# Waits by bank at two stages, cross attention reordered, cached rotary keys turned by VectorE, and another order of ScalarE's splits in each block's first span

## What is computed

```python
xp = xp + 0.5 * swiglu_ffn(xp, ffn1_norm, ffn1_w_gate, ffn1_w_up, ffn1_w_down)      # D_FF = 2816
q_lat, q_rope, c_kv, k_rope, u = mixer_project(xp, pos_p, mix_norm, w_in, ...)       # input projection
o_lat = mla_attend(q_lat, q_rope, pos_p, ((c_kv, k_rope, pos_p),))                   # 8 heads, latent 256, rope 32
xp = xp + mix_output(o_lat, u_ext, w_v_up, conv_w, conv_b, conv_ln_g, conv_ln_b, w_out)
...
past_c = cache_kv_latent[page_table].reshape(8, 4096, 256)      # paged cache of the decode requests
past_kr = cache_k_rope[page_table].reshape(8, 4096, 32)         # rotary keys of the cache
# scores of a decode step: q_lat . c + q_rope . kr, over 4096 cached and 4 new keys
s = (einsum('bqhc,btc->bhqt', ql, c) + einsum('bqhr,btr->bhqt', qr, kr)) * ATTN_SCALE
...
xp = xp + cross_attend(xp, cross_norm, w_cq, mk, mv, w_co)      # 4 heads of 256; decode rows use cached mem_k, mem_v
xp = xp + 0.5 * swiglu_ffn(xp, ffn2_norm, ffn2_w_gate, ffn2_w_up, ffn2_w_down)
y = rmsnorm(xp, final_norm)
```

## Time and profile before

| what | value |
|---|---|
| median of three runs | 2448.7 us (2446.03 to 2457.05) |
| the profiled execution's own time | 2448.1 us |
| its span | 2446.3 us |
| TensorE busy | 2393.6 us (98%) |
| TensorE weight loads busy | 2250.0 us (92%) |
| VectorE busy | 1462.0 us (60%) |
| ScalarE busy | 953.6 us (39%) |
| GpSimd busy | 1149.6 us (47%) |
| mean granted TensorE clock | 0.995 |

### The profile page before, as it was taken

One profiled execution on the slowest core, in us unless ns is written; L12 is line 12 of the kernel. 1 busy time (PEld: TensorE's weight loads), 2 busy tenths in 40 slices (PEclk: granted clock), 3 DMA queues, 4 the chain that ended last, 5 costly groups with the idle time before them and its releaser, 6 DMA issues.

```text
span 2446.3 us, 48239 instructions
## 1 busy us (share of the span) xinstructions
PE 2393.6 (98%) x18415; PEld 2250.0 (92%) x18415; DVE 1462.0 (60%) x2672; ACT 953.6 (39%) x2015; POOL 1149.6 (47%) x832
## 2 busy tenths in 40 slices
PE   7999999999999999999999999999999999999998
PEld 7999999999999888666677999789999999999998
DVE  6644545468784756866777761444654545456786
ACT  7323333343332334666443330432532333334335
POOL 2647777787833251002212422013465777777770
PEclk9999999999999999999999999999999999999999
DMA  4112323245423123006564312431112232325432
GB/s 127 35 53 92 104 91 104 91 150 163 123 60 120 47 60 98 1 1 267 198 247 122 122 43 77 154 106 47 41 53 61 87 109 86 109 86 170 141 105 80
DMA packets 191279, 246.57 MB, mean 101 GB/s; under 512 B 9768, under 2 KB 152457, under 8 KB 186262
## 3 DMA queue, kind: packets, MB, share of 16 engines
q1 hardware_dynamic: 187007, 205.11, 27.0%
q0 software_dynamic: 3584, 37.75, 3.9%
q10 hardware_dynamic: 543, 1.69, 0.2%
HBM read 197.93 MB, written 42.80 MB: 98 GB/s over the span
## 4 chain that ended last, share of the span: by engine, by line
PE 58%; DVE 3%; ACT 1%; issue 1%; POOL 0%; ACTq 0%; DVEq 0%
PE ps L1445 6%; PE ps L1440 6%; PE ps L1444 6%; PE ps L422 4%; PE ps L425 4%; PE ps L426 4%; PE ps L2785 3%; PE ps L1547 2%; PE ps L1551 2%; PE ps L1550 2%; PE ps L2815 2%; PE ps L2830 1%; PE ps L2797 1%; PE ps L3155 1%; PE ps L3009 1%; PE ps L3135 1%
## 5 line engine op out<-in xcount | busy, mean ns | idle before, releaser
L1440 PE MATMUL ps<-op_hi_S,home_hi 128*128 128x264 f32 x1280 | 364.2, 285 | 0.0
L1445 PE MATMUL ps<-op_hi_S,home_lo 128*128 128x264 f32 x1280 | 364.0, 284 | 0.0
L1444 PE MATMUL ps<-op_lo_S,home_hi 128*128 128x264 f32 x1280 | 363.6, 284 | 0.0
L1838 DVE TENSOR_TENSOR ps<-st_copy,ps 128x264 f32<-128x264 f32 x196 | 85.6, 437 | 333.5 <-PE ps L1445 294.1
L1440 PE MATMUL ps<-op_hi_A,home_hi 128*128 128x264 f32 x960 | 273.4, 285 | 0.0
L1444 PE MATMUL ps<-op_lo_A,home_hi 128*128 128x264 f32 x960 | 272.9, 284 | 0.0
L1445 PE MATMUL ps<-op_hi_A,home_lo 128*128 128x264 f32 x960 | 272.8, 284 | 0.0
L2447 POOL CAST w_hi<-w_raw 128x1024 fp32r<-128x1024 f32 x40 | 49.0, 1224 | 431.7 <-PE ps L422 146.9
L1975 POOL TENSOR_TENSOR home_lo<-home_v,home_hi 128x512 fp32r<-128x512 f32 x160 | 212.2, 1337 | 74.3 <-ACT home_hi L1567 74.3
L1445 PEld LDWEIGHTS ps<-op_hi_S,home_lo 128*128 128x128 f32 x1280 | 240.9, 188 | 0.0
L1444 PEld LDWEIGHTS ps<-op_lo_S,home_hi 128*128 128x128 f32 x1280 | 240.9, 188 | 0.0
(11 more groups left out here) (444 smaller groups left out, 6518.0 us busy)
## 6 DMA issues: line engine op xcount, KB each, us to landing
g_v<-g_keep SPq DMA_DIRECT2D x56, 528.0 KB, 3.7
f_raw<-in_ffn_w_gate SPq DMA_DIRECT2D x44, 512.0 KB, 4.0
f_raw<-in_ffn_w_up SPq DMA_DIRECT2D x44, 512.0 KB, 4.1
g_keep<-st SPq DMA_DIRECT2D x16, 1320.0 KB, 6.0
f_raw<-in_ffn_w_down SPq DMA_DIRECT2D x28, 512.0 KB, 3.9
g_keep<-st SPq DMA_DIRECT2D x16, 528.0 KB, 2.7
span_raw<-in_ffn_w_down SPq DMA_DIRECT2D x16, 512.0 KB, 5.6
ring<-in_cache_mem_k SPq DMA_DIRECT2D x16, 512.0 KB, 4.2
```

The source lines that it names most:

```text
L1440: mm = pe.matmul(out, w, xhi[:, k, q], start=self.STARTS[unit] and k == 0, stop=False, skip_group_check=True)
L1444: pe.matmul(out, w, xlo[:, k, q], start=False, stop=False, skip_group_check=True)
L1445: mm = pe.matmul(out, lo, xhi[:, k, q], start=False, stop=self.STOPS[unit] and k == KH - 1, skip_group_check=True)
L1838: dve.tensor_tensor(out, a, b, op).then_inc(self.evicted, 1)
```

## The change

Five edits.

1. First span of each FFN: ScalarE makes g_hi of product 3 before the two span_hi splits, and stays one product ahead in span 0; VectorE makes g_lo of product 3 behind the seventh tile of product 0 instead of behind the fourth.
2. The first units of the input projection wait, tile by tile, for the last add on the bank that they use.
3. The first units of the query projection do likewise.
4. Cross attention starts with the scores of steps 0 and 1, each waiting for less, and turns the first probabilities between the two halves of c_turned(0). At the end, the transposes of co_s come ahead of x_values(15), which goes to bank 5.
5. In decode attention, VectorE transposes kr_nat in 32x32 blocks into kr_t, of which there are two; the group of TensorE transposes and its ScalarE copy go. A block transpose leaves the positions in another layout, so the rope scores are 16 matmuls of 128 columns instead of four of 512.

```diff
-        TURNS = 9
-        TURN_OF = [(0, 0), (0, 1), (0, 2), (0, 3), None, (1, 0), (1, 1), (1, 2), (1, 3)]
+        TURNS = 8
+        TURN_OF = [(ch, j) for ch in range(2) for j in range(4)]
...
+        def rope_turned(h):
+            return v_dve, QT + h + 1
...
+        def x_bank(j):
+            return 5 if j == X_STEPS - 1 else 3
...
+            def last_of_bank(self, bank):
+                return self.tile_added(self.LAST, max(i for i in range(self.N_TILES) if self.TILE_BANKS[i] == bank))
...
                     if last:
+                        operand_high(0, 3)
                         span_high(0, 4)
                         span_high(0, 5)
...
-                        if p < 4:
+                        if p < 3 and first:
+                            operand_high(q, p + 4)
+                        elif p < 4 and not first:
                             operand_high(q, p + 3)
-                        elif not last:
+                        elif p >= 4 and not last:
                             operand_high(q + 1, p - 4)
...
-                            if j == 4 and p < 4:
+                            if p < 4 and j == (7 if first and p == 0 else 4):
                                 operand_low(q, p + 3)
...
+            def second_taken(self, mb, tt):
+                return self.taken, self.o + 2 * NTT + NTT * KC + NTT * mb + tt + 1
...
                 if h >= 2:
-                    pool.wait_ge(turned_pe, TURNS * (h - 2) + 5)
+                    pool.wait_ge(*rope_turned(h - 2))
...
-                    pe.wait_ge(z_dve, NTT * (2 * m + s) + tt + 1)
+                    if m == 0:
+                        pe.wait_ge(*ffn1.last_of_bank(NTT * s + tt))
+                    else:
+                        pe.wait_ge(z_dve, NTT * (2 * m + s) + tt + 1)
...
-                for part, turns in enumerate(((0, 1, 2, 3), (4,), (5, 6, 7, 8))):
-                    for i in turns:
+                rope = kr_t[h % 2][:, :].rearrange("p (n j x) -> p j n x", n=4, j=4)
+                for ch in range(2):
+                    for i in range(4 * ch, 4 * ch + 4):
                         pe.wait_ge(*key_turn_taken(h, i))
                     for j in range(4):
...
+                    if ch == 0:
+                        pe.wait_ge(*rope_turned(h))
+                        for r in range(4):
+                            for j in range(4):
+                                out = ps[32 * j:32 * j + NS, 4 + d, :].rearrange("p (n r x) -> p r n x", n=4, r=4)
+                                pe.matmul(out[:, r], qr_rows[:, b, r, :], rope[:, j], start=False, stop=False)
...
-                    pe.wait_ge(xq_dve, NTT * (2 * m + s) + tt + 1)
+                    if first:
+                        pe.wait_ge(*w_out.second_taken(KC - 2 + s, tt))
+                    else:
+                        pe.wait_ge(xq_dve, NTT * (2 * m + s) + tt + 1)
...
-                if j:
+                if j and j < X_STEPS - 1:
                     pe.wait_ge(xo_dve, j)
...
+            pe.wait_ge(xq_dve, 2 * NTT + NTT * (KC - 1))
+            x_scores(0)
+            pe.wait_ge(xq_dve, 2 * NTT + NTT * (KC - 1) + 1)
+            x_scores(1)
             pe.wait_ge(xq_dve, 2 * NTT + NTT * KC)
-            x_scores(0)
             c_turned(0, 0)
+            x_turned(0)
             c_turned(0, 1)
-            x_scores(1)
...
-            x_values(X_STEPS - 1)
             pe.wait_ge(co_done, 1)
             for c in range(2):
                 pe.transpose(ps[:, 6 + c, 0:P], co_s[:, c * P:(c + 1) * P], ident).then_inc(coh_pe, 1)
+            x_values(X_STEPS - 1)
...
+                if 1 <= h < UNITS:
+                    rope_keys_turned(h)
```

More of the change, by code:

```diff
@@ L352, in hybrid_layer @@
         c_t = at("c_t", [P, 2, 4, 512], raw_off)
-        kr_t = at("kr_t", [P, 512], raw_off + 16384)
+        kr_t = [at("kr_t%d" % n, [P, 512], off) for n, off in enumerate((o_off + 16 * SEQ, raw_off + 16384))]
         p_tr = at("p_tr", [P, 2, 512], raw_off + 18432)
@@ L1728, in span @@
                     last = isinstance(q, int) and q == SPANS - 1
+                    first = isinstance(q, int) and q == 0
                     for p in range(7):
-                        if p < 4:
+                        if p < 3 and first:
+                            operand_high(q, p + 4)
+                        elif p < 4 and not first:
                             operand_high(q, p + 3)
-                        elif not last:
+                        elif p >= 4 and not last:
                             operand_high(q + 1, p - 4)
@@ L1904, in span @@
                 def span(q):
-                    last = isinstance(q, int) and q == SPANS - 1
+                    first, last = isinstance(q, int) and q == 0, isinstance(q, int) and q == SPANS - 1
                     for p in range(7):
                         for j in range(8):
-                            if j == 4 and p < 4:
+                            if p < 4 and j == (7 if first and p == 0 else 4):
                                 operand_low(q, p + 3)
-                            elif j == 4 and not last:
+                            elif p >= 4 and j == 4 and not last:
                                 operand_low(q + 1, p - 4)
@@ L2809, in keys_turned @@
                 for n in range(4):
-                    if TURN_OF[i] is None:
-                        keys = kr_nat[:, h % 2, n * P:(n + 1) * P]
-                    else:
-                        ch, j = TURN_OF[i]
-                        keys = c_nat[slot(h)[0]][:, 4 * n + j, ch * P:(ch + 1) * P]
+                    ch, j = TURN_OF[i]
+                    keys = c_nat[slot(h)[0]][:, 4 * n + j, ch * P:(ch + 1) * P]
                     mm = pe.transpose(ps[:, g % 3, n * P:(n + 1) * P], keys, ident)
@@ L3121, in _ @@
             for s in range(2):
-                query_unit(0, s)
+                query_unit(0, s, first=True)
                 cross_n.sums_after(pe, s)
@@ L3212, in _ @@
                     c_turned(b, 0)
-                x_turned(j)
+                if j:
+                    x_turned(j)
                 if j % 2 == 0 and b < DEC_BATCH:
@@ L3478, in _ @@
                         keys_taken(h, i)
-                    if h % 2 == 0 and 2 <= h <= UNITS and i in (5, 6, 8):
-                        d_exp(h // 2 - 1, {5: 0, 6: 1, 8: 2}[i])
+                    if h % 2 == 0 and 2 <= h <= UNITS and i >= 5:
+                        d_exp(h // 2 - 1, i - 5)
                     if h % 2 == 1 and 3 <= h <= UNITS + 1 and i == 3:
@@ L3913, in _, with rope_keys_turned @@
             steps.wait()
+            def rope_keys_turned(h):
+                dve.wait_ge(kr_in[h % 2], 16 * (h // 2 + 1))
+                if h >= 2:
+                    dve.wait_ge(sc_mm, h - 1)
+                dve.transpose(kr_t[h % 2][:, :], kr_nat[:, h % 2, :]).then_inc(v_dve, 1)
             def d_maxima(h):
@@ L4155, in _ @@
                     c_maxima(b)
+                if j == X_STEPS - 1:
+                    dve.wait_ge(cpv_done, 2 * DEC_BATCH)
+                    dve.tensor_copy(co_s[:, :], ps[:, 7, 0:N_MEM]).then_inc(co_done, 1)
                 if j:
                     x_low(j - 1)
-            dve.wait_ge(cpv_done, 2 * DEC_BATCH)
-            dve.tensor_copy(co_s[:, :], ps[:, 7, 0:N_MEM]).then_inc(co_done, 1)
-            x_low(X_STEPS - 1)
             for c in range(2):
```

32 lines of the change are left out of this document (13 added, 19 removed).

## The result

The changed kernel takes 2431.7 us (median of four runs, 2430.24 to 2432.38) against 2449.7; the ratio is 0.9929, with an interval from 0.9917 to 0.9940. A second set of five runs gave 2431.5 us and 0.9936 (0.9922 to 0.9949); by medians the gain is 17.9 us in the first set and 16.0 in the second. The forecast was 2430.6 us. The profiled execution's span is 2430.5 us where it was 2446.3.

The account below looks back on a forecast made before the run. TensorE, busy 98% of the span, was taken as the bound. Terms 7.1 + 1.8 + 2.0 + 0.8 + 1.5 + 7.0 − 1.9 − 0.5 = 17.8 us off 2448.1, plus 0.3 for the median, gave 2430.6 us; range 2424 to 2443.

Parts of the forecast that it names:

- the query projection and cross attention: Query projection's starting wait goes, 2.0 us; cross attention gains 0.8 at its start and 1.5 at its end.
- First span: Both FFN blocks: two TensorE waits go, 5.5 us, plus 1.6 from one half-clock stretch; 7.1 us together.
- Input projection: TensorE starts its first tiles earlier; gain taken as 1.8 us, bounds −1.7 and 4.0.
- the blocks beside GpSimd are slow: Input projection: VectorE's low blocks beside GpSimd's CAST are slow, so TensorE waits about 1.2 us in the middle.
- only 2.1 us can be gained before PE waits for it: Input projection: weights landing by DMA at an unmoved time, then their low part, cap the gain at 2.1 us.
- The half-clock stretch that the prediction left out of its sum: Input projection's start: a half-clock stretch of 1.7 us behind the old wait, seen as possible gain but not counted.
- Decode: Decode attention: 7.0 us from dropped TensorE transposes, less 1.9 for narrow matmuls and 0.5 for VectorE's transposes.
- The narrow matmuls: Decode rope scores: 16 matmuls of 128 columns replace four of 512, costing 1.9 us, half the 3.8 us bound.
- the bound from 32-column rows: Decode rope scores: 32 records at 34 ns take 1.09 us, +0.24 a unit, +3.8 us in all.
- The early units: Decode: 0.5 us lost, for three units without memory work and first units where VectorE waits for landed keys.
- the price that the prediction weighs there: Decode: skill's 81 ns per 128-column matmul would make 32 records 2.6 us and lose 28 us; prediction set it aside.
- The prediction's estimate of 1.2 us: Decode: VectorE's block transpose estimated from four bf16 128x128 transposes, 0.3 beyond the slack, losing some 3 to 4 us.

Follow-up runs that it names:

- the rope part: Only VectorE's block transposes of the rotary keys, with the narrow rope matmuls, put on the kernel before: 2448.9 us, ratio 0.9994.
- the cast later: Changed kernel with GpSimd's CAST of the second unit's input-projection weights held until VectorE has made the last low block: 2430.8 us.

## Why the prediction was right, point by point

The time fell inside the range and 1.1 us from the forecast, and each wait that the prediction named went. But the closeness of the number is partly luck. Measured alone, the query projection and cross attention gave 6.4 us where 4.3 was forecast (2.0 + 0.8 + 1.5), and the rope part 0.3 where 4.6 was (7.0 − 1.9 − 0.5), which lies outside its interval of −1.0 to 3.9. In the sum the two cancel.

**First span.** 7.1 forecast; 7.4 alone, 4.4 + 2.9 = 7.3 by the traces. Both steps held: order on ScalarE frees g_hi, and half-clock time goes with the waits. It is not one stretch with the first wait, though: that wait had one in three of the four traces that keep it, and the second in two of four (2238 and 2244), which is 2.1 us on average where the prediction counted 1.6.

**Input projection.** 1.8 forecast, 1.8 by the profiled trace, 2.1 alone with an interval from −0.5 to 4.4. The reason was half right. That the blocks beside GpSimd are slow and cost some 1.2 us was right to a tenth, and the run with the cast later shows it. The step that named what comes late next, "only 2.1 us can be gained before PE waits for it", named the weights: TensorE does wait for them by 0.23 us in one trace of the changed kernel and not at all in the other, and once the low blocks are fast the sums of squares stand before them. The half-clock stretch that the prediction left out of its sum is 1.3 us on average (three of four traces), and by the clocks of all executions the lower clock accounts for all that this part gave alone.

**Query projection and cross attention.** 2.0, 0.8 and 1.5 forecast; 2.2, 1.1 and 1.7 in the trace.

**Decode.** 4.6 forecast. By the trace 1.8, and 5.2 when the 3.4 us of low clock are added back; by the clocks of all executions of the rope part alone 3.4. The one trace with the edit and no lower clock here, that of the cast later, also gives 3.4 (196.25 us from the last row named "before decode" in the table to unit 16's probabilities, and 199.69 before), but one unit's scores took 1.0 us longer in it, for which the profile shows no cause. So 4.6 lies between what was measured, and nothing here fixes it closer. Two terms were off and partly cancel. The narrow matmuls cost 0.3 us and not 1.9 (0.02 us a unit): the bound from 32-column rows said nothing of 128 columns in four groups. The early units cost 1.2 us (waits of 1.17, 0.48, 1.06 and 1.35 us where there were 0.30, 1.08, 0.92 and two of 0.30) and not 0.5: in even units the transpose stands before the row maxima, for which I had read the slack from later units. Moved behind them it gains nothing, since ScalarE's probabilities are late there next. With both terms as measured the sum is 7.0 − 0.3 − 1.2 = 5.5.

One reading of the prediction is wrong. Four transposes of 128 columns take 0.44 us, but the trace has one record for each of them (512 records for 16 × 8 × 4 transposes of latent keys), not two: they are 110 ns apart and not 55, and so say nothing against the price that the prediction weighs there. What does is measured only now: 27 ns a record, 54 a matmul, for the 16 narrow matmuls.

The block transpose was taken at 0.7 and is 0.706. The Trainium skill's "Vector Engine (DVE) Microarchitecture Reference", section 3.8 "The reshape front-end and per-opcode configuration", says that the block transpose sustains one element per cycle per lane; this trace agrees so far as it takes 0.706 us, beside 0.69 for plain passes over the same 128x512. The prediction's estimate of 1.2 us, from the bf16 figure of the Trainium skill's "VectorE: DVE Perf Modes", section "The three transpose paths", is not borne out.

**What was not forecast.** The stretch at 1100 cost the profiled execution 3.4 us, 0.5 were lost in its first 43 us and 1.0 in its last 200, and the missing v_all wait gave 1.2 back. So the median came out within 1.1 us of the forecast partly because such pieces offset the terms that were too careful; as the medians of the changed kernel in the two sets and of the kernel before in four (2447.6 to 2449.7) show, some 2 us are all the accuracy that a sum of this kind can have here.

## What to carry to other kernels

Follow a removed wait to the next two engines that it pulls forward, not only to the next transfer: 1.2 us freed by one edit came back in full as a wait for VectorE's adds. Order narrow matmuls so that successive ones go to different column groups; the exchange of two loops was worth 19 us. And where a clock can fall at a wait, compare medians of many executions for the time and traces for the mechanism: a single trace can carry 1.7 or 3.4 us that belong to no edit. Where the granted clock of every execution is on record, take its loss off before you credit an edit with the rest.

## What the runs showed of the hardware that I had not expected

- The same program has its half-clock stretches in different places from one execution to the next, costing 1.7 or 3.4 us each but for the last, 8.5 to 16.9 us in all over the fourteen traces. Where a wait was removed, no trace had one any more. The runs of the kernel before spread from 2445.8 to 2457.1 us.
- Two more differences come and go without any edit: the wait of 1.2 us for v_all near 911 to 918, and a stop of 1.43 us at 2231 put down to "issue" in one trace.
- GpSimd's CAST of 128x1024 takes 1.04 us alone, and 4.79 us when it falls beside VectorE's adds of squares (the row at 733.74).
- 128-column fp32 matmuls with a weight load each run at 27 ns a record (two records a matmul) into alternating column groups, and at about 65 ns four in a row into one. The Trainium skill's "TensorE: Matmul & The Clock Gate", section "The mechanism", lets tiles at different positions overlap, which the first figure agrees with; what four matmuls in a row at the same position cost it does not say.
